# Level scores of two gated linear branches, one or two to a visit of the matmul engine, in a two-layer hybrid decoder trunk

## What is computed

```python
def chunk_gated_linear(q, k, v, log_g):
    # o_t = q_t^T S_t with S_t = diag(exp(log_g_t)) S_{t-1} + k_t v_t^T, chunks of 64 positions
    ...
        o_inter = jnp.einsum('bhtk,bhkv->bhtv', qb * jnp.exp(gb), s_st)
        diff = gb[:, :, :, None, :] - gb[:, :, None, :, :]
        decay = jnp.exp(jnp.where(causal[:, :, None], diff, -jnp.inf))
        att = jnp.einsum('bhtk,bhsk,bhtsk->bhts', qb, kb, decay)
        o = o_inter + jnp.einsum('bhts,bhsv->bhtv', att, vb)
        s_new = (jnp.exp(g_end)[..., None] * s_st
                 + jnp.einsum('bhsk,bhsv->bhkv', kb * jnp.exp(g_end[:, :, None, :] - gb), vb))
```

## Time and profile before

| what | us |
|---|---|
| median of three runs (1949.28 to 1950.25) | 1950.16 |
| the profiled execution, its own time | 1949.91 |
| its span, first to last instruction | 1948.1 |
| TensorE matmul busy in the span | 1931.3 |
| GpSimd | 1127.9 |
| VectorE | 1249.7 |
| ScalarE | 961.8 |

### The profile page before, as it was taken

The page is one execution under the profiler, slowest core; times in us unless marked ns, Lnnn a source line. Parts: engine busy times, 40 slices in busy tenths (PEclk is TensorE's granted clock), DMA queues, the critical chain, the costliest instruction groups (busy, mean ns, idle before and its releaser), DMA issues.

```text
span 1948.1 us, 33275 instructions
## 1 busy us (share of the span) xinstructions
PE 1931.3 (99%) x12707; PEld 1641.5 (84%) x12707; DVE 1249.7 (64%) x1909; ACT 961.8 (49%) x1665; POOL 1127.9 (58%) x1356
## 2 busy tenths in 40 slices
PE   7999999999999999999999999999999999999998
PEld 6788788888888889999887887888898888999997
DVE  5888778856145766767358786787641556667661
ACT  6754645345445644444456647353554655344334
POOL 4565564956834555766565555467576355566653
PEclk9999999999999999999999999999999999999999
DMA  6423233333422333333342233333343233333332
GB/s 187 119 73 85 82 83 88 87 109 107 148 82 81 99 99 102 99 103 98 98 102 79 72 87 82 81 83 87 120 130 124 66 98 95 111 104 98 103 98 81
DMA packets 196091, 191.41 MB, mean 98 GB/s; under 512 B 23834, under 2 KB 186204, under 8 KB 195548
## 3 DMA queue, kind: packets, MB, share of 16 engines
q1 hardware_dynamic: 194780, 187.19, 32.7%
q10 hardware_dynamic: 1152, 2.10, 0.3%
HBM read 185.04 MB, written 3.15 MB: 97 GB/s over the span
## 4 chain that ended last, share of the span: by engine, by line
PE 95%; ACT 2%; DVE 2%; DMA 1%; issue 0%; SPq 0%; POOL 0%; DVEq 0%; ACTq 0%
PE gemm L701 73%; PE mix L701 20%; DMA w_raw<-in_w_in_dram 1%; DVE work L1974 0%; DVE work L1965 0%; PE mix L1283 0%; DMA work<-in_norm_mix_dram 0%; DVE sums_raw L1965 0%; PE mix L944 0%; PE mix L1178 0%; ACT w_hi L1429 0%; ACT work L1819 0%; DMA w_raw<-in_mlp_w_dram 0%; PE mix L877 0%; ACT work_split L1579 0%
## 5 line engine op out<-in xcount | busy, mean ns | idle before, releaser
L694 POOL TENSOR_TENSOR w_lo<-w_raw,w_hi 128x256 fp32r<-128x256 f32 x676 | 584.8, 865 | 793.0 <-ACT w_hi L1429 793.0
L695 POOL TENSOR_TENSOR w_lo<-w_raw,w_hi 128x256 fp32r<-128x256 f32 x676 | 595.8, 881 | 0.0
L701 PE MATMUL gemm<-h_hi,w_hi 128*128 128x512 f32 x1248 | 493.7, 396 | 0.5 <-DVE h_lo L1974 0.5
L701 PE MATMUL gemm<-h_lo,w_hi 128*128 128x512 f32 x1248 | 486.2, 390 | 0.0
L701 PE MATMUL gemm<-h_hi,w_lo 128*128 128x512 f32 x1248 | 486.1, 390 | 0.0
L701 PE MATMUL gemm<-work_split,w_hi 128*128 128x512 f32 (+1 forms) x1552 | 446.9, 373 | 0.3
L1429 ACT ACTIVATE w_hi<-w_raw 128x512 fp32r<-128x512 f32 x676 | 380.0, 622 | 62.8 <-DMA w_raw<-in_w_in_dram 24.6
L701 PEld LDWEIGHTS gemm<-work_split,w_hi 128*128 128x128 f32 x1552 | 281.6, 189 | 51.0 <-DVE work_split L1974 1.1
L701 PE MATMUL gemm<-work_split,w_lo 128*128 128x512 f32 (+1 forms) x776 | 288.5, 372 | 0.0
L701 PEld LDWEIGHTS gemm<-h_hi,w_hi 128*128 128x128 f32 x1248 | 234.3, 188 | 56.7 <-issue 6.6
L701 PEld LDWEIGHTS gemm<-h_hi,w_lo 128*128 128x128 f32 x1248 | 234.3, 188 | 49.5
(11 more groups left out here) (372 smaller groups left out, 2792.9 us busy)
## 6 DMA issues: line engine op xcount, KB each, us to landing
w_raw<-in_mlp_w_dram SPq DMA_DIRECT2D x256, 256.0 KB, 2.7
w_raw<-in_w_in_dram SPq DMA_DIRECT2D x208, 256.0 KB, 2.7
w_raw<-in_xattn_w_kv_dram SPq DMA_DIRECT2D x64, 256.0 KB, 3.0
w_raw<-in_w_branch_dram SPq DMA_DIRECT2D x32, 256.0 KB, 2.7
w_raw<-in_w_out_dram SPq DMA_DIRECT2D x32, 256.0 KB, 2.7
w_raw<-in_xattn_w_q_dram SPq DMA_DIRECT2D x32, 256.0 KB, 2.8
w_raw<-in_xattn_w_o_dram SPq DMA_DIRECT2D x32, 256.0 KB, 2.7
w_raw<-in_w_in_dram SPq DMA_DIRECT2D x32, 128.0 KB, 3.5
```

The lines of the kernel that those rows point to most:

```text
L694: pool.tensor_tensor(lo[:, 0:half], raw[:, 0:half], hi[:, 0:half].bitcast(F32), ALU.subtract)
L695: pool.tensor_tensor(lo[:, half:], raw[:, half:], hi[:, half:].bitcast(F32), ALU.subtract).then_inc(split_ready, 1)
L701: return pe.matmul(o, w, a, start=start, stop=stop, skip_group_check=True)
```

## The change

TensorE: levels 1 to 6 of either branch are issued in three visits of two levels instead of six visits of one. Each pair stands where its second level stood. VectorE: `level_mul` of a pair are put together ahead of the picks of the pair before. In GLA, `conv(2)`, `merge(3, 1)`, `pick(5)`, `decayed`, `pick(6)` and `conv(3)` now follow each other in this order. ScalarE, GpSimd and SyncE keep their programs, and no instruction is added or dropped.

```diff
@@ TensorE
-                pe.wait_ge(*of_layer(gl.gate_in, 2))
-                scores(hg, 1)
                 block = parts("r_g", *H)
                 some(block, 2)
+                pe.wait_ge(*of_layer(gl.gate_in, 2))
+                scores(hg, 1)
                 scores(hg, 2)
                 rest(block)
-                scores(hg, 3)
                 block = gate_parts(3, 0)
                 some(block, 2)
+                scores(hg, 3)
                 scores(hg, 4)
                 rest(block)
-                scores(hg, 5)
                 block = parts("m_q", *H)
                 some(block, 2)
+                scores(hg, 5)
                 scores(hg, 6)
...
                 scores(gl, 0)
                 rest(block)
-                scores(gl, 1)
                 block = parts("m_o", *H)
                 some(block, 3)
+                scores(gl, 1)
                 scores(gl, 2)
                 rest(block)
                 branch_gemm(3, 0)
-                scores(gl, 3)
                 block = gate_parts(3, 1)
                 some(block, 3)
+                scores(gl, 3)
                 scores(gl, 4)
                 rest(block)
                 branch_gemm(3, 1)
                 block = gate_parts(3, 2)
-                some(block, 1)
+                rest(block)
                 scores(gl, 5)
-                rest(block)
                 scores(gl, 6)
@@ VectorE, HGRN
-                pick(hg, 1)
                 level_diff(hg, 4)
                 gate_out("g_r", gl.GR)
                 level_mul(hg, 3)
+                level_mul(hg, 4)
+                pick(hg, 1)
                 pick(hg, 2)
                 level_diff(hg, 5)
-                level_mul(hg, 4)
-                pick(hg, 3)
                 level_diff(hg, 6)
                 gate_out("r_g", hg.GR)
                 level_mul(hg, 5)
+                level_mul(hg, 6)
+                pick(hg, 3)
                 pick(hg, 4)
-                level_mul(hg, 6)
                 last_decay(hg)
+                decayed(hg)
                 pick(hg, 5)
-                decayed(hg)
                 pick(hg, 6)
@@ VectorE, GLA
                 level_mul(gl, 1)
+                level_mul(gl, 2)
                 pick(gl, 0)
                 level_diff(gl, 3)
-                pick(gl, 1)
+                level_diff(gl, 4)
                 do(dve.tensor_copy(pr(17), Ur[:, S5_T, :]))
...
-                level_mul(gl, 2)
-                level_diff(gl, 4)
-                pick(gl, 2)
...
                 level_mul(gl, 3)
                 level_mul(gl, 4)
+                pick(gl, 1)
+                pick(gl, 2)
                 level_diff(gl, 5)
                 level_diff(gl, 6)
-                pick(gl, 3)
                 merge(3, 0)
                 conv(0)
                 conv(1)
-                pick(gl, 4)
                 level_mul(gl, 5)
                 level_mul(gl, 6)
+                pick(gl, 3)
+                pick(gl, 4)
...
                 last_decay(gl)
                 conv(2)
+                merge(3, 1)
                 pick(gl, 5)
                 decayed(gl)
-                merge(3, 1)
+                pick(gl, 6)
                 conv(3)
                 silu_of(0)
                 silu_of(1)
-                pick(gl, 6)
                 decayed_queries(gl)
```

More of the change, by code:

```diff
@@ L1019, in _ @@
                 rest(block)
+                block = parts("r_g", *H)
+                some(block, 2)
                 pe.wait_ge(*of_layer(gl.gate_in, 2))
                 scores(hg, 1)
-                block = parts("r_g", *H)
-                some(block, 2)
                 scores(hg, 2)
                 rest(block)
-                scores(hg, 3)
                 block = gate_parts(3, 0)
                 some(block, 2)
+                scores(hg, 3)
                 scores(hg, 4)
                 rest(block)
-                scores(hg, 5)
                 block = parts("m_q", *H)
                 some(block, 2)
+                scores(hg, 5)
                 scores(hg, 6)
```

## The result

The changed kernel takes 1952.46 us (median; 1950.81 to 1954.32) against 1950.18 for the kernel before, measured beside it. The ratio is 1.0013, with an interval of 1.0007 to 1.0019: slower by 2.3 us, where 0.2 less was forecast. It lies 0.26 us above the top of the range given. The profiled execution took 1953.25 us (span 1951.4).

A forecast was written before the change was run, and what follows sets the result against it. TensorE, busy 99% of the span, was taken as the bound. Saving 2.33 us a layer, mostly eaten by a new 2.4 us wait, left 0.2 us off 1949.91; with 0.25 for the median, 1949.9 us, range 1947.6 to 1950.8.

The forecast's parts named there:

- The saving: TensorE's level scores: three fewer visits in HGRN (0.96 us) and GLA (1.02), plus GLA level 3's 0.35 wait: 2.33 us a layer.
- the old wait of 0.23: TensorE's stop before `state_in(gl)` in the kernel before, 0.55 us against 0.32 elsewhere, where VectorE's pick of level 6 ends last.
- The rival that a level keeps its price inside a pair: A pair's second level still pays 0.32 or 0.34 us, only the 0.35 is saved: 1953.2 us, slower; chance 0.07.
- The new wait: TensorE at `state_in(gl)` stands still 2.4 us a layer, released by ScalarE's `kt_copy` queued behind `conv(3)`'s tanh.
- the chain: From GLA's pair of 5 and 6: pick 5, `decayed`, pick 6, `conv(3)`, tanh, `kt_copy`, then `state_in(gl)` at 211.24.
- the step that carried over the old time of that queue: VectorE from `level_mul` 3 at 174.47: old 27.82 us, plus 1.53, less 2.13, puts it before pick 5 at 201.69.
- The one size that I called unknown: VectorE's `conv(3)` beside GpSimd, taken as 4.00 us; low end 2.93, giving 1947.8 us.
- the rival of the harder GpSimd: Each of `conv(3)`'s four instructions sits out a whole GpSimd instruction: 6.13 us, 2.1 more a layer, 1954.2 us; chance 0.03.
- the sum itself: `state_in(gl)` starts 0.12 us earlier a layer despite the 2.4 us stop; over two layers 0.2 us off 1949.91.
- a falling clock in its last paragraph: Sign against the forecast: the granted clock falls behind the wait at `state_in(gl)`; no size or chance given.
- the whole saving arrives: Rival: `state_in(gl)` does not have to wait, so 5.1 us go: 1945.1 us, faster; chance 0.13.

The follow-up runs named there:

- the copy-first version: Changed kernel, but ScalarE copies GLA's transposed keys (`kt_copy`) ahead of the tanh of `conv(3)` instead of behind it: 1944.12 us, ratio 0.9968.
- HGRN's half alone: Kernel before, with only HGRN's three pairs on TensorE and its VectorE order of picks and products, GLA as before: 1948.06 us, ratio 0.9988.
- GLA's with the copy: Changed kernel with HGRN's half undone and `kt_copy` ahead of the tanh of `conv(3)`: 1946.86 us, ratio 0.9981.
- the version with 1.9 us of wait: Changed kernel, but on VectorE `conv(3)` stands ahead of pick 6 instead of behind it: 1949.17 us, ratio 0.9996.
- the one with 0.8: Changed kernel with `kt_copy` ahead of `conv(3)`'s tanh and three of `conv(3)`'s four VectorE instructions ahead of pick 6: 1946.01 us, ratio 0.9978.

## Why the prediction was wrong

**The saving** was right in its mechanism, and a little low. Forecast were 2.33 us a layer and the old wait of 0.23, 2.56; the copy-first version shows 2.91. From one `outputs(gl)` to the other, HGRN's half alone saves 1.10 us instead of 0.96 (959.63 us a layer), and GLA's with the copy 1.76 instead of 1.60 (958.97). One HGRN pair read as above saves 0.34 instead of 0.32; the rest I have not traced. The rival that a level keeps its price inside a pair falls with this; the second level costs its 32 matmuls only.

**The new wait** was at the forecast place, with the forecast releaser, and 0.5 us too small. From the first matmul of the pair of 5 and 6 to `state_in`, the chain was put at 211.24 - 201.52 = 9.72 us; it took 211.83 - 201.66 = 10.17. TensorE's own way between the two was put at 7.28, and is 209.08 - 201.83 = 7.25 in the copy-first version, where nothing stops it. So TensorE stands still for 2.92 us instead of 2.44. Two terms make the difference. Pick 5 starts 1.10 us behind the pair's first matmul instead of 0.83: VectorE did not wait there for the scores, as I had said it would, since its own queue got there later, 1.07 us behind the forecast 201.69. `level_mul` 3 began at 174.69, only 0.22 behind its forecast, but `level_mul` 5 and 6 then took 195.85 - 191.30 = 4.55 us, where the kernel before shows 196.04 - 192.31 = 3.73; so the step that carried over the old time of that queue was 0.85 short, 0.82 of it there. VectorE's timeline, the start of `level_mul` 3, the start of 5 and what follows 6, in the changed kernel, then the last two in the kernel before:

```profile
174.69 0.43 DVE L1964 TENSOR_TENSOR work<-work 128x256 f32<-128x256 f32 x1 [1.24 <-ACT work L1539]
...
191.30 0.84 DVE L1964 TENSOR_TENSOR work<-work 128x256 f32<-128x256 f32 x1
...
195.85 1.46 DVE L2090 COPY_PREDICATED work<-masks_sb,mix 128x512 f32<-128x512 int32 x2
...
192.31 0.79 DVE L1965 TENSOR_TENSOR work<-work 128x256 f32<-128x256 f32 x1
...
196.04 0.69 DVE L1965 TENSOR_TENSOR work<-work 128x512 f32<-128x512 f32 x1
```

The second term: `decayed` took 0.96 us instead of the 0.69 of the earlier trace rows; no run was made to ask why either took longer. The one size that I called unknown, `conv(3)`, came out at 210.51 - 206.56 = 3.95 where I took 4.00, so the rival of the harder GpSimd falls too. Its 6.13 had each of the four instructions sit out a whole GpSimd instruction, and no run shows that: wherever the versions of the changed kernel leave `conv(3)` in one piece, it takes 3.2 to 4.3 us.

Up to here the steps give 2.92 - 2.91, a layer that is as long as before, where 0.12 less was forecast.

**The step that failed** is the sum itself: "So it stands still for 2.4 us and starts 0.12 earlier than before", multiplied by two, prices the wait at its own length. Behind this wait TensorE's work ran at 0.50 for some 3 us in both layers, and 1.5 us went in each, 3.0 in all. The prediction named a falling clock in its last paragraph as something that would make it wrong, but gave it neither a price nor a chance, so the sum put it at nothing and the range left no room for it. The rows that it read gave no price. In the trace of the kernel before, TensorE stands still for more than 1.4 us in two places only: in front of its first matmul, with a clock of 1.00 behind it, and behind its last at the end of the span, where the clock falls to 0.50 and no matmul is left to be slowed. The first matmul in TensorE's timeline, and the two stretches:

```profile
7.46 0.48 PE L964 MATMUL gemm<-consts_sb,work 128*128 128x128 f32 x1 [7.46 <-DMA work<-in_norm_mix_dram]
...
7.00:10.50 3.50, 3.04 (x14) 3.04 (x15) 0.17 (x1) 0.63 (x1) 0.81 (x2) 1.00 1.08 386
...
1946.00:1948.10 2.10, 0.00 (x0) 0.00 (x0) 0.00 (x0) 0.00 (x0) 0.00 (x0) 0.50 0.52 194
```

So the rows left open whether the clock would fall; the term should have stood in the sum with bounds, nothing on one side and on the other a stretch of the stream at the 0.50 that the end of the span shows, for whose length these rows give no number, and the range should have reached up by it. The changed kernel's trace has the numbers: a mean of 0.72 over six us is 3.4 us at 0.50, in which two gemm matmuls start 215.01 - 214.59 = 0.42 us apart instead of 0.227, and in the versions whose clock fell the marks are 1.3 to 1.6 us further apart, a little under half of such a stretch.

**The rival "the whole saving arrives"** was rejected rightly: the copy was really behind `conv(3)`. What it needed was not a shorter chain, as I had put it, but one line moved on ScalarE, and then it arrives: 1945.1 forecast for it, 1944.12 measured.

## What to carry to other kernels

Before a reordering of one engine is judged, follow each in-order queue that it feeds: here a copy that was ready at 206.2 stood behind a tanh that VectorE had made late, and moving that one line turned a loss of 2.3 us into a gain of 5.9. Price a new stop of a TensorE that is otherwise busy at its length plus a fall of the clock, here 1.5 us, which came behind nine of twelve idles of 1.9 to 4.4 us and behind neither of two of 0.8; a stop that can't be removed is covered by moving independent matmuls in front of it, as here one part of 12 more, with which the time was 1944.65 us.

## What had not been expected of the hardware

The clock's fall did not follow the idle time alone: 3.09 us of idling left it at 1.00 in one layer and 1.92 us brought it to 0.50 in another, once at no price and once at the full one (12.48 and 14.00 us between the marks, 12.45 without a wait). A kernel with such stops may spread more for it, though no run tests that by itself: the version with 1.9 us of wait ran from 1947.44 to 1951.91 us, the one with 0.8 from 1945.06 to 1947.24, both in eleven runs.
